# Two pairs of ffn chunks per stage computed as 2x2 block products with seven products instead of eight

## The reference, cut to what matters

```python
def swiglu(h, w_in, w_out):
    gate, up = jnp.split(h @ w_in, 2, axis=-1)
    return (jax.nn.silu(gate) * up) @ w_out
x = x + 0.5 * swiglu(rmsnorm(x, g), w_in, w_out)     # x (256, 1024), w_in (1024, 5632), w_out (2816, 1024)
```

## Time and profile before

| | us |
|---|---|
| median of 3 runs | 2125.68 (2125.38 to 2128.99) |
| span of the profiled execution | 2123.9 |
| PE busy | 2075.8, 98% |
| DVE busy | 1196.0, 56% |
| ACT busy | 1031.3, 49% |
| mean granted TensorE clock | 0.997 |
| DMA | 359.98 MB, mean 169 GB/s |

### The profile page before, as it was taken

One profiled execution on the slowest core, in us unless ns is written; L12 is line 12 of the kernel. 1 busy time (PEld: TensorE's weight loads), 2 busy tenths in 40 slices (PEclk: granted clock), 3 DMA queues, 4 the chain that ended last, 5 costly groups with the idle time before them and its releaser, 6 DMA issues.

```text
span 2123.9 us, 26075 instructions
## 1 busy us (share of the span) xinstructions
PE 2075.8 (98%) x10491; PEld 1744.1 (82%) x10491; DVE 1196.0 (56%) x1542; ACT 1031.3 (49%) x1359; POOL 71.6 (3%) x113
## 2 busy tenths in 40 slices
PE   8999999999999999999999999999999999989999
PEld 6887988888888878888888889888888787877887
DVE  5545687555645576654565446655555555765454
ACT  6435436444544468644454444544455444764443
POOL 2000000000000000000000000007001000000000
PEclk9999999999999999999999999999999999989999
DMA  8553425655555442565555544586647654114553
GB/s 260 191 195 120 159 91 173 212 179 191 175 196 193 140 159 80 178 218 179 178 178 180 197 158 159 188 244 195 179 138 173 204 191 168 62 57 162 178 180 117
DMA packets 259880, 359.98 MB, mean 169 GB/s; under 512 B 19582, under 2 KB 200234, under 8 KB 259760
## 3 DMA queue, kind: packets, MB, share of 16 engines
q1 hardware_dynamic: 256800, 351.57, 50.4%
q0 software_dynamic: 2016, 4.95, 1.5%
q10 hardware_dynamic: 944, 1.79, 0.3%
...
HBM read 356.70 MB, written 1.57 MB: 169 GB/s over the span
## 4 chain that ended last, share of the span: by engine, by line
PE 87%; DVE 6%; ACT 4%; issue 1%; DMA 1%; ACTq 0%; DVEq 0%; SPq 0%
PE bank L421 17%; PE bank L423 16%; PE bank L422 16%; PE acc L718 6%; PE acc L720 6%; PE acc L719 6%; PE bank L416 2%; PE bank L417 2%; PE bank L418 2%; PE tr L699 2%; DVE w_lo_ L445 2%; ACT w_hi_ L435 1%; PE acc L748 1%; PE acc L750 1%; PE acc L749 1%
## 5 line engine op out<-in xcount | busy, mean ns | idle before, releaser
L445 DVE TENSOR_TENSOR w_lo_<-raw_in,w_hi_ 128x2048 fp32r<-128x2048 f32 (+1 forms) x333 | 574.1, 1732 | 214.0 <-ACT w_hi_ L435 213.7
L421 PE MATMUL bank<-w_hi_,xt_hi_ 128*128 128x512 f32 x1648 | 658.4, 400 | 2.6 <-DVE xt_lo_ L545 2.4
L423 PE MATMUL bank<-w_hi_,xt_lo_ 128*128 128x512 f32 x1648 | 643.6, 391 | 0.0
L422 PE MATMUL bank<-w_lo_,xt_hi_ 128*128 128x512 f32 x1648 | 642.4, 390 | 0.0
L435 ACT ACTIVATE w_hi_<-raw_in 128x2048 fp32r<-128x2048 f32 (+1 forms) x333 | 481.7, 1461 | 64.7 <-DMA raw_in<-ffn_w_in 31.3
L844 DVE TENSOR_TENSOR wo_lo_<-raw_out,wo_hi_ 128x2048 fp32r<-128x2048 f32 x80 | 183.8, 2297 | 484.2 <-ACT wo_hi_ L798 484.2
L423 PEld LDWEIGHTS bank<-w_hi_,xt_lo_ 128*128 128x128 f32 x1648 | 309.4, 188 | 66.3
L421 PEld LDWEIGHTS bank<-w_hi_,xt_hi_ 128*128 128x128 f32 x1648 | 310.0, 188 | 64.9 <-issue 4.8
L422 PEld LDWEIGHTS bank<-w_lo_,xt_hi_ 128*128 128x128 f32 x1648 | 310.2, 188 | 59.0
L798 ACT ACTIVATE wo_hi_<-raw_out 128x2048 fp32r<-128x2048 f32 x80 | 153.3, 1916 | 369.7 <-PE acc L720 359.3
L718 PE MATMUL acc<-wo_hi_,ht_hi_ 128*128 128x512 f32 x576 | 224.3, 389 | 2.7 <-DVE ht_lo_ L831 2.7
...
## 6 DMA issues: line engine op xcount, KB each, us to landing
raw_in<-ffn_w_in SPq DMA_DIRECT2D x352, 512.0 KB, 4.9
raw_out<-ffn_w_out SPq DMA_DIRECT2D x88, 1024.0 KB, 5.0
raw_in<-hg_w_in SPq DMA_DIRECT2D x16, 1024.0 KB, 5.2
raw_in<-fox_w_in SPq DMA_DIRECT2D x16, 1024.0 KB, 5.4
raw_in<-conv_w_in SPq DMA_DIRECT2D x12, 1024.0 KB, 5.1
raw_in<-hg_w_out SPq DMA_DIRECT2D x4, 1024.0 KB, 5.0
raw_in<-fox_w_out SPq DMA_DIRECT2D x4, 1024.0 KB, 5.2
raw_in<-conv_w_out SPq DMA_DIRECT2D x4, 1024.0 KB, 5.0
```

Of the source, the lines that this page charges most:

```text
L421: mm(o, xt_hi[:, k, tok], wh[:, par, k, 0:w], start=first, stop=False)
L422: mm(o, xt_hi[:, k, tok], wl[:, par, k, 0:w], start=False, stop=False)
L423: last = mm(o, xt_lo[:, k, tok], wh[:, par, k, 0:w], start=False, stop=end)
L445: dve.e.tensor_tensor(g.piece(g.wl, n, half, k), raw, g.piece(g.wh, n, half, k).bitcast(F32), ALU.subtract).then_inc(g.w_lo, 4 if k is Non ...
```

## The change

In six of the eight ffn stages (all but f5 and f6) chunks 2 and 3 are taken together, and chunks 6 and 7; chunks 4 and 5 between them stay plain ("N" in the code, a pair is "S"). For a pair the 256 tokens by 1024 rows of x and the 1024 rows by 1024 columns of `w_in` (512 gate, 512 up columns) are seen as 2x2 blocks, and gate and up are formed from seven block products of 12 matmuls each, instead of eight:

- Four blocks of raw weights, b11, b12, b21, b22 (512 rows by 512 columns, 1 MB, one DMA each), are loaded into the arena. The seven weight operands are B11, B21 and B22 as loaded, and T3 = b12 + b22, T2 = b11 + T3, T4 = b21 + T2, T1 = T2 - b22. Each is split by ACT and DVE like a half of a plain chunk, into a ring of four places (before: the same memory, by chunk parity). T2, T4, T1 are sums on DVE, 128x2048; T3 is one too in the first pairs of f0, f1, f3 and f7, and in the other eight pairs it is an accumulating DMA issued by GpSimd (Pool), which reads b22's columns from memory again and adds them to b12.
- Four sums of x blocks are formed once per stage by DVE (`dve_x_add`, after chunk 0) and split by ACT and DVE (`act_x_sum`, `dve_x_sum`, in chunk 1, ahead of `read(1)` on both).
- The seven products use the banks `bank0`, `bank1` and `tr1`. ACT copies the first out, and DVE combines them by seven operations of 128x512; `h` of both chunks comes from one silu and one product of 512 columns per tile.
- `second` of the chunks before a pair is postponed: PE's order in a pair (chunks c, c+1, with q = c-1) is B11, B21, `turn(q)`, T2, T1, `second(q-1)`, T3, B22, T4, `second(q)`. After a pair each `turn` and `second` is one chunk late until chunk 5 or 9.
- SP loads b11 and b12, then b22 and b21, ahead of the second plain chunk of a stage (in f0 from the start, in f1, f3 and f7 after the first addition of the mixer before), and later pairs' blocks during the pair before, as its splits and sums are done; for f2 and f4 that is the stage before.
- The masks of the hgrn mixer are loaded during f0 instead of at the start, since their memory holds `up1` in a pair. The two small loads of the fox mixer move from f2 to the start of fox. The rest of the diff renumbers semaphores.

The diff, cut to what the text speaks of:

```diff
+PAIRED = {f: (2, 6) for f in (0, 1, 2, 3, 4, 7)}
+PAIRS = [(f, c) for f in range(8) for c in PAIRED.get(f, ())]
...
+def _count_operands():
+    first, before, used, products = [], [], [], 0
+    starts = {N0[S_FFN[f]] + c for f, c in PAIRS}
+    for n in range(N_ALL + 1):
+        first.append(len(used))
+        before.append(products)
+        if n in starts:
+            used += [products + i + 1 for i in range(7)]
+            products += 7
+        elif n - 1 not in starts:
+            used += [products + 2] * 2
+            products += 2
+    return first, before, used
+OPN, PDN, USED = _count_operands()
+T3_BY_POOL = [p for p, (f, c) in enumerate(PAIRS) if c != PAIRED[f][0] or f in (2, 4)]
+PAIR_CHUNKS = {N0[S_FFN[f]] + c + i for f, c in PAIRS for i in range(2)}
...
+                if form == "N":
+                    if before == "S":
+                        i += 1
+                        chunk(i)
+                        w_out_chunk(c - 1)
+                        todo = c
+                        continue
+                    if c == 0 and after == "S":
+                        w_out_chunk(0)
+                        todo = 1
+                    while todo < c:
+                        w_out_chunk(todo)
+                        todo += 1
+                    if c == 0 and here:
+                        block(p, 3)
+                        block(p, 2)
+                    i += 1
+                    chunk(i)
+                else:
+                    while todo < c:
+                        w_out_chunk(todo)
+                        todo += 1
+                    if next_pair_early(p):
+                        for which in (0, 1, 3, 2):
+                            block(p + 1, which)
+                    w_out_chunk(c)
+                    todo = c + 1
+                    p += 1
...
+def pe_pair(g, pe, f, p, turn, second, q, pending):
+    s, c = S_FFN[f], PAIRS[p][1]
+    n, u, j = N0[S_FFN[f]] + c, U[S_FFN[f]], list(PAIRED).index(f)
+    x = lambda half, t: tuple(v[:, 4 * half:4 * half + 4, t * P:(t + 1) * P] for v in (g.xt_hi_, g.xt_lo_))
+    a, y, z = g.bank[0], g.bank[1], g.tr[1]
+    def product(bank, of_x, i):
+        op = OPN[n] + i
+        pe.wait_ge(g.w_lo, 4 * op + 4)
+        hi, lo = of_x
+        wh, wl, mm = g.wh[:, op % 4], g.wl[:, op % 4], pe.e.matmul
+        for k in range(KT // 2):
+            mm(bank[:], hi[:, k], wh[:, k], start=k == 0, stop=False)
+            mm(bank[:], hi[:, k], wl[:, k], start=False, stop=False)
+            last = mm(bank[:], lo[:, k], wh[:, k], start=False, stop=k == KT // 2 - 1)
+        last.then_inc(g.prod, 1)
+    def summed(i):
+        pe.wait_ge(g.ss_lo, 4 * j + i + 1)
+        return g.sah[i], g.sal[i]
+    pe.wait_ge(g.xt_lo, 16 * u + 16)
+    pe.wait_ge(g.st_c, 7 * p)
+    product(z, x(0, 0), B11)
+    pe.wait_ge(g.h, 22 * f + 2 * q + 2)
+    product(y, x(1, 0), B21)
+    turn(q)
+    product(a, summed(A_S2), T2)
+    pe.wait_ge(g.st_cp, p + 1)
+    product(z, summed(A_S1), T1)
+    second(pending)
+    pe.wait_ge(g.st_c, 7 * p + 1)
+    product(y, summed(A_S3), T3)
+    pe.wait_ge(g.st_c, 7 * p + 2)
+    product(a, summed(A_S4), B22)
+    pe.wait_ge(g.st_c, 7 * p + 3)
+    product(z, x(1, 1), T4)
+    second(q)
...
         for t in range(NT):
             if slot_c:
                 slot_c(t * KT)
-            if c:
+            if before == "S":
+                pe.wait_ge(g.st_c, 7 * PAIRS.index((f, c - 2)) + 6 - t)
+            elif c:
                 pe.wait_ge(g.h, 22 * f + 2 * (c - 1) + t + 1)
             pe_product(g, pe, n0 + c, t, g.bank[t], u, slot=slot_c)
             if t == 0 and c:
-                turn(c - 1)
-        if 0 < c < NCH - 1:
+                if before == "S" and after is None:
+                    second(c - 2)
+                    turn(c - 1)
+                elif before == "S":
+                    turn(c - 2)
+                else:
+                    if pending is not None:
+                        second(pending)
+                    turn(c - 1)
+        if before == "S" and after is None:
+            pending = None
+        elif before == "S":
+            second(c - 2)
+            turn(c - 1)
+            pending = c - 1
+        elif after == "S":
+            pending = c - 1
+        elif 0 < c < NCH - 1:
             second(c - 1)
+            pending = None
+        before = form
...
+def dve_block_sum(g, dve, p, i):
+    f, c = PAIRS[p]
+    op = OPN[N0[S_FFN[f]] + c]
+    b11, b12, b21, b22 = g.blocks
+    if i == T3:
+        if p in T3_BY_POOL:
+            return
+        dve.wait_ge(g.b12_in, 16 * (p + 1))
+        dve.wait_ge(g.b22_in, 16 * (p + 1))
+        dve.e.tensor_tensor(b12, b12, b22, ALU.add).then_inc(g.st_t3, 1)
+    elif i == T2:
+        wait_t3(g, dve, p)
+        dve.wait_ge(g.w_lo, 4 * (op + B11) + 4)
+        dve.e.tensor_tensor(b11, b11, b12, ALU.add).then_inc(g.st_add, 1)
+    elif i == T4:
+        dve.wait_ge(g.w_lo, 4 * (op + B21) + 4)
+        dve.wait_ge(g.st_add, 3 * p + 1)
+        dve.e.tensor_tensor(b21, b21, b11, ALU.add).then_inc(g.st_add, 1)
+    else:
+        dve.wait_ge(g.b22_in, 16 * (p + 1))
+        dve.wait_ge(g.w_lo, 4 * (op + T2) + 4)
+        dve.wait_ge(g.st_add, 3 * p + 2)
+        dve.e.tensor_tensor(b11, b11, b22, ALU.subtract).then_inc(g.st_add, 1)
...
+        if owner == f and p in T3_BY_POOL:
+            pool.wait_ge(g.b12_in, 16 * (p + 1))
+            pool.e.dma_start(g.blocks[1], w[:, KT // 2:, 1, c * FC:(c + 2) * FC], accum_op=ALU.add).then_inc(g.t3_in, 16)
...
+    def pair(p, q, pending):
+        c, n = PAIRS[p][1], N0[s] + PAIRS[p][1]
+        act_block(g, act, p, T2)
+        turn(pending)
+        weights_out(pending)
+        act_block(g, act, p, T1)
+        act.wait_ge(g.prod, PDN[n] + 1)
+        if p:
+            act.wait_ge(g.silu, 22 * PAIRS[p - 1][0] + 2 * PAIRS[p - 1][1] + 4)
+        act.e.activation(g.p1s, g.tr[1][:], ACT.Copy).then_inc(g.st_cp, 1)
+        act_block(g, act, p, T3)
...
+        act_split(g, act, n + 2, 0)
+        turn(q)
+        weights_out(q)
+        act_split(g, act, n + 2, 1)
+        act.wait_ge(g.st_c, 7 * p + 7)
+        act.wait_ge(g.h, 22 * f + 2 * q + 2)
+        act.wait_ge(g.squares, 4 * R[s] + 4)
+        act.wait_ge(g.rstd, 2 * R[s] + 2)
+        act.e.activation(g.sq[:], g.p1s, ACT.Silu, scale=g.rstd_[:, 1:2]).then_inc(g.silu, 2)
...
+            p = PAIRS.index((f, c + 1))
+            act_block(g, act, p, B11)
+            if pending is not None:
+                turn(pending)
+                weights_out(pending)
+            elif before == "S":
+                weights_out(c - 2)
+            act_block(g, act, p, B21)
+            read(0)
+            if before == "S":
+                turn(c - 2)
+            if c == PAIRED[f][0] - 1:
+                for i in range(4):
+                    act_x_sum(g, act, f, i)
+            read(1)
+            pending = c - 1
+        elif pending is not None or before == "S":
...
+    def pair(p, q, pending):
+        c, n, first_one = PAIRS[p][1], N0[s] + PAIRS[p][1], PAIRS[p][1] == PAIRED[f][0]
+        a, y, z = g.bank[0], g.bank[1], g.tr[1]
+        dve_block(g, dve, p, T2)
+        dve_block_sum(g, dve, p, T1)
+        turn(pending)
+        weights_out(pending)
+        dve_block(g, dve, p, T1)
+        dve.wait_ge(g.prod, PDN[n] + 2)
+        dve.wait_ge(g.st_cp, p + 1)
+        dve.wait_ge(g.h, 22 * f + 2 * q + 2)
+        dve.e.tensor_tensor(g.silu0, y[:], g.p1s, ALU.add).then_inc(g.st_c, 1)
+        dve_block(g, dve, p, T3)
+        dve.wait_ge(g.prod, PDN[n] + 3)
+        dve.wait_ge(g.st_c, 7 * p + 1)
+        dve.e.tensor_tensor(g.p1s, a[:], g.p1s, ALU.add).then_inc(g.st_c, 1)
+        dve_block(g, dve, p, B22)
+        dve.wait_ge(g.prod, PDN[n] + 4)
+        dve.wait_ge(g.st_c, 7 * p + 2)
+        dve.wait_ge(g.h_turned, 12 * f + (0 if first_one else PAIRS[p - 1][1] + 2))
+        dve.e.tensor_tensor(g.up0, z[:], g.p1s, ALU.add).then_inc(g.st_c, 1)
+        dve_block(g, dve, p, T4)
+        dve_split(g, dve, n + 2, 0)
+        turn(q)
+        weights_out(q)
+        dve.wait_ge(g.prod, PDN[n] + 5)
+        dve.wait_ge(g.st_c, 7 * p + 3)
+        dve.e.scalar_tensor_tensor(g.up1, y[:], -1.0, g.up0, ALU.mult, ALU.subtract).then_inc(g.st_c, 1)
+        dve.e.tensor_tensor(g.p1s, y[:], g.p1s, ALU.add).then_inc(g.st_c, 1)
+        dve_split(g, dve, n + 2, 1)
+        dve.wait_ge(g.prod, PDN[n] + 6)
+        dve.wait_ge(g.st_c, 7 * p + 4)
+        dve.e.scalar_tensor_tensor(g.up0, a[:], -1.0, g.up0, ALU.mult, ALU.subtract).then_inc(g.st_c, 1)
+        dve.wait_ge(g.silu, 22 * f + 2 * c + 2)
+        dve.wait_ge(g.st_c, 7 * p + 6)
+        dve.wait_ge(g.rstd, 2 * R[s] + 2)
+        dve.e.scalar_tensor_tensor(g.up0, g.up0, g.rstd_[:, 0:1], g.silu0, ALU.mult, ALU.mult).then_inc(g.h, 2)
+        dve.wait_ge(g.prod, PDN[n] + 7)
+        dve.e.tensor_tensor(g.p1s, z[:], g.p1s, ALU.add).then_inc(g.st_c, 1)
```

(54 more changed lines are left out.)

352 lines of the change are left out of this document (264 added, 88 removed).

## The result

The changed kernel takes **2224.52 us** (median of 4 runs, 2221.57 to 2228.15), the kernel before beside it 2127.34 us (4 runs): ratio **1.0459, 95% interval 1.0444 to 1.0474**, 97.2 us slower. The forecast was 2192.3; the time lies 32.2 us above it and 2.5 us above the end of the range. The direction was right, the size was not.

A forecast was written before the change was run, and what follows sets the result against it. PE, busy 98% of the span, was taken as the bound. The profiled 2123.9 us, plus 66.6 for waits less matmuls saved, plus 1.8 to the median gave 2192 us, 3.1% slower; range 2165 to 2222.

The forecast's parts named there:

- The gain: Gate and up of each pair: 84 matmuls instead of 96, 2.72 us saved, 32.6 us for 12 pairs.
- Wait 1: Every pair, at turn(q): PE waits 2.47 us for DVE's ht_lo of chunk q-1.
- wait 3: Once a stage, first pair's B21: PE waits for h(1,1); 1.9 us in f2 and f4, 5.4 to 5.9 elsewhere.
- Wait 2: Every pair, ahead of T1's product: PE waits 1.21 us for DVE's low part of T1.
- Wait 4: Once a stage, at second(8): PE waits 3.6 us for the low part of w_out 8, loaded late.
- The heads: Chunk 1's weights land late behind the blocks: 5.4 us more in f0, 1.1 in f7.
- What cost nothing: Accumulating DMA, taken as about 11 us and hidden; also DMA room, hgrn masks; fox loads 0 to 1 us.
- rival (d): Accumulating DMA far slower than a third of a plain one, holding T2 in eight pairs: +40 us, 2232; 5%.
- The sum: Six stages at +5.5 us, 33.0, plus 33.6 for first-pair waits and late chunk 1: +66.6 us.
- rival (b): PE's clock falls to half in first pairs of four stages: 8 to 20 us more, 2205 as middle; 25%.
- four six-us waits: First pairs of f0, f1, f3, f7: PE waits near 6 us at the second product, B21.

The follow-up runs named there:

- sums_apart: A later kernel (reordered pairs at chunks 3 and 7, loads moved) with the split x sums' pieces 512 elements apart instead of 128: 2106.33 us, ratio 0.9899.
- t3_pool: The changed kernel with the sum T3 made by the accumulating DMA in all twelve pairs instead of eight: 2236.14 us, ratio 1.0511.
- filler: The changed kernel with 318 matmuls that nobody reads put where TensorE waits: 2211.08 us, ratio 1.0399.

## Why the prediction was wrong in size and right in direction

**The gain.** 144 matmuls fewer, as forecast. Its price of 0.2267 us held for the products with x but not for all of the pair: four of seven products have a split x sum as stationary operand, and their matmuls start further apart. Product T1 (eleven intervals from the first line to the second) and a stretch of the second product behind it (twelve intervals), at the same clock:

```profile
625.21 0.39 PE L838 MATMUL tr<-w_hi_,sums_split 128*128 128x512 f32 x1
...
627.78 0.39 PE L840 MATMUL tr<-w_hi_,sums_split 128*128 128x512 f32 x1
...
629.39 0.40 PE L903 MATMUL acc<-wo_hi_,ht_hi_ 128*128 128x512 f32 x1
...
632.12 0.39 PE L903 MATMUL acc<-wo_hi_,ht_hi_ 128*128 128x512 f32 x1
```

(627.78 - 625.21) / 11 = 0.2336 against (632.12 - 629.39) / 12 = 0.2275. That is 48 x 12 x 0.0065 = 3.7 us more in twelve pairs (the expectation of sums_apart counted 60 products); why is open.

**Wait 1** was forecast at 2.47 in 12 places. It is 2.31 shown, 2.47 with the 0.16 that the view leaves out, in all six second pairs, and 2.13 and 2.17 in the first pairs of f2 and f4. In the other first pairs it is 0.6 or less, since the long wait 3 and the slow product behind it gave DVE time. **Wait 2**, forecast 1.21, is 1.03 shown (1.19) in four places, 0.49 in a fifth, and hidden by the slow clock in the other seven. **Wait 3**, forecast 1.9 and 5.4 to 5.9: 2.13 shown in f2 and f4, 5.7 to 5.8 in the others. **Wait 4**, forecast 3.6: 3.7 to 3.9 in four stages, 4.6 and 5.1 in f2 and f4. **The heads**, forecast 5.4 in f0 and 1.1 in f7: 4.9 and 2.05. Mechanism and place were right for every wait, and the lengths within half a microsecond for most; wait 4 in f2 and f4 (by 1.0 and 1.5), f7's head (by 0.9) and the waits that others or the slow clock hid were not.

**What cost nothing.** The accumulating DMA lands in 13.5 us where 11 were taken, and no PE wait names it: rival (d) is refuted, as far as its duration goes. Its bytes are another matter (t3_pool).

**The step that failed** is the price of a wait. The sum gave each its idle time alone and left the clock to rival (b), priced at 8 to 20 us for the four six-us waits, with 25%. The trace's clock records have 18 falls in the six paired stages, 89 us at 0.50 in all; most stand behind waits of 2 to 4 us. For 14 of these 89 us TensorE was idle anyway; the other 75 at half speed cost an estimated 37. Rival (b) was thus right as a mechanism and mis-sized: it counted the four longest waits, where 22 of 2 us and over had to be counted, 18 of them with a fall.

The account is made for the two profiled executions, since the waits are theirs. Their spans are 102.9 us apart, where the medians are 97.2: the profiled execution of the changed kernel was its slowest, and had the lowest mean clock (0.975, against 0.979 in the fastest). In it: -32.6 for the matmuls removed; +84.2 of idle time shown in the six stages beyond the kernel before's 8.6; some 7.5 for the restarts behind 30 waits (0.16 and about 0.1 each); +3.7 for the matmuls of the sums. That makes 62.8 and leaves **40.1 for the clock**. It is what is left over, but the clock records give nearly the same: the 37 above and some 5 for the falls in fox and f6. The forecast's +66.6 is -32.6 and 99.2 of waits, of which 91.7 are there; 40.1 + 3.7 - 7.5 = 36.3 is what it lacked against this execution. Against the medians it lacked 30.6, and the other 1.6 of the 32.2 are the kernel before's own median, 2127.3 this time where 2125.7 was taken. The filler run took away some 30 us of the clock's share and put 15 of waits in their place. That the miss was no larger is in part luck: waits that the slow clock or a longer wait hid made the idle time 7.5 us less than forecast, and so covered part of it.

The rule cited with rival (b), the Trainium skill, "TensorE: Matmul & The Clock Gate", section "HAM oscillation — how this bites in real kernels", speaks of long gaps between bursts. The runs agree that gaps bring the low clock, but it came here behind waits of 1.9 to 2.3 us too, between stretches that were otherwise full; behind twelve equal ones it came seven times. And the trace of before, which the prediction called in agreement in the one place where PE starves, has another: PE waits 3.13 us in fox, and the clock stays at 1.00.
